# Recurrence scan: K and B in one stationary tile, V over U, 128x128 turns

## The reference, cut to what matters

```python
def step(state, inp):
    r_t, w_t, k_t, v_t, a_t, b_t = inp
    sa = jnp.einsum('bhvk,bhk->bhv', state, a_t)
    state = (state * w_t[:, :, None, :] + sa[..., None] * b_t[:, :, None, :]
             + v_t[..., None] * k_t[:, :, None, :])
    return state, jnp.einsum('bhvk,bhk->bhv', state, r_t)
...
y = rwkv7_scan(rh, heads(decay), kh, vh, -kk, kk * ah)
```

## Time and profile before

| what | value |
|---|---|
| median of 3 runs | 4486.77 us (4481.82 to 4492.76) |
| the profiled execution, its own time | 4486.94 us |
| span of the profiled execution | 4485.2 us |
| PE busy | 4139.9 us, 92% of the span |
| the two scans | 456 to 678 us and 1793.5 to 2015.5 us, 222 us each |

### The profile page before, as it was taken

One profiled execution on the slowest core, in us unless ns is written; L12 is line 12 of the kernel. 1 busy time (PEld: TensorE's weight loads), 2 busy tenths in 40 slices (PEclk: granted clock), 3 DMA queues, 4 the chain that ended last, 5 costly groups with the idle time before them and its releaser, 6 DMA issues.

```text
span 4485.2 us, 74522 instructions
## 1 busy us (share of the span) xinstructions
PE 4139.9 (92%) x32508; PEld 3239.7 (72%) x32508; DVE 1952.9 (44%) x2997; ACT 1514.7 (34%) x2697; POOL 548.8 (12%) x384
## 2 busy tenths in 40 slices
PE   7998779899998999789899989987899999999999
PEld 5676776677776776776677767755788888667877
DVE  5536335455345536335455344357432232443232
ACT  3533233333333533233333343257221121343221
POOL 1215101011002216001011001012000000150000
PEclk9999899999998999899999999999999999999999
DMA  4122002244322132003244321100111111101222
GB/s 161 39 104 71 31 4 104 80 170 173 136 82 103 48 104 66 32 9 114 93 169 169 128 80 43 52 24 1 38 62 62 63 65 57 57 6 66 94 94 85
DMA packets 97684, 351.74 MB, mean 78 GB/s; under 512 B 10064, under 2 KB 13648, under 8 KB 95952
## 3 DMA queue, kind: packets, MB, share of 16 engines
q1 hardware_dynamic: 86480, 313.02, 20.2%
q10 hardware_dynamic: 10880, 33.96, 2.1%
HBM read 332.26 MB, written 14.68 MB: 77 GB/s over the span
## 4 chain that ended last, share of the span: by engine, by line
PE 81%; DVE 8%; issue 3%; POOL 3%; ACT 3%; DMA 0%; ACTq 0%; DVEq 0%; SPq 0%; POOLq 0%
PE ps L350 20%; PE ps L351 19%; PE ps L353 19%; PE ps L1373 7%; PE ps L2414 1%; PE ps L1932 1%; DVE wlo L307 1%; DVE sml L2489 1%; POOL e L2948 1%; PE ps L391 1%; ACT whi L297 1%; PE ps L2861 1%; POOL dd L1215 1%; POOL ops L1231 1%; PE ps L885 1%
## 5 line engine op out<-in xcount | busy, mean ns | idle before, releaser
L307 DVE TENSOR_TENSOR wlo<-ring,whi 128x1024 fp32r<-128x1024 f32 x494 | 622.6, 1261 | 1827.8 <-ACT whi L297 1827.5
L297 ACT CAST whi<-ring 128x1024 fp32r<-128x1024 f32 x494 | 517.2, 1048 | 2069.2 <-PE ps L353 1791.7
L350 PE MATMUL ps<-h_hi,whi 128*128 128x512 f32 x1424 | 592.8, 416 | 21.6 <-DVE h_lo L461 10.2
L351 PE MATMUL ps<-h_lo,whi 128*128 128x512 f32 x1424 | 566.4, 398 | 0.0
L353 PE MATMUL ps<-h_hi,wlo 128*128 128x512 f32 x1424 | 566.0, 397 | 0.0
L350 PE MATMUL ps<-hm_hi,whi 128*128 128x512 f32 (+1 forms) x1408 | 514.6, 365 | 15.9 <-DVE hm_lo L464 14.4
L351 PE MATMUL ps<-hm_lo,whi 128*128 128x512 f32 (+1 forms) x1408 | 481.0, 357 | 0.0
L353 PE MATMUL ps<-hm_hi,wlo 128*128 128x512 f32 (+1 forms) x1408 | 418.9, 355 | 0.0
L350 PEld LDWEIGHTS ps<-h_hi,whi 128*128 128x128 f32 x1424 | 271.3, 191 | 141.8 <-issue 49.5
L350 PE MATMUL ps<-ac_hi,whi 128*128 128x512 f32 x880 | 330.5, 376 | 3.4 <-DVE wlo L307 3.4
L350 PEld LDWEIGHTS ps<-hm_hi,whi 128*128 128x128 f32 x1408 | 267.2, 190 | 85.9 <-DVE hm_lo L464 19.4
(11 more groups left out here) (386 smaller groups left out, 7240.6 us busy)
## 6 DMA issues: line engine op xcount, KB each, us to landing
ring<-in_w SPq DMA_DIRECT2D x590, 512.0 KB, 3.3
h_spill<-h ACTq DMA_DIRECT2D x2, 2048.0 KB, 6.7
x_spill<-x ACTq DMA_DIRECT2D x2, 2048.0 KB, 13.8
m_spill<-m ACTq DMA_DIRECT2D x2, 2048.0 KB, 9.8
h_again<-h_spill ACTq DMA_DIRECT2D x2, 2048.0 KB, 9.0
ma<-m_spill ACTq DMA_DIRECT2D x2, 2048.0 KB, 9.9
x<-x_spill ACTq DMA_DIRECT2D x2, 2048.0 KB, 9.9
x<-in_x SPq DMA_DIRECT2D x4, 512.0 KB, 7.8
```

Source lines behind the costliest of these rows:

```text
L297: self.A.copy(self.hi[k % 2][:], raw).then_inc(self.s_cut_hi.h, 1)
L307: self.V.tensor_tensor(self.lo[k % 2][:], raw, self.hi[k % 2][:].bitcast(F32), ALU.subtract).then_inc(self.s_cut_lo.h, 1)
L350: T.matmul(ps[:, b, 0:cw], hi, xh(q, c0, cw), start=q == 0, stop=False, skip_group_check=True)
L351: T.matmul(ps[:, b, 0:cw], hi, xl(q, c0, cw), start=False, stop=False, skip_group_check=True)
```

## The change

K and B are stored next to each other, chunk by chunk, in `kb`, so that one stationary tile of 64 rows by 128 columns holds both. One product then gives K and B with R and A for one head half, at place 0, in place of `ba` and `ka`. V moves to the fourth part of `ops` and A to the fifth. `stacked` contracts over 128 rows: the turned K and B stand under each other in `kbt`, and V and U in `vu`, so `st` and `yy` are one product each. `turned` turns whole 128x128 tiles with PE's transpose; the V tile holds two chunks, and is turned for each of them. `turned` and `stacked` and the new first product issue all their matmuls in one step of the weave. `tb` moves from place 1 of the old chunk to place 7 of the new one. PSUM banks 1 and 3 change roles. ACT gains the copy `ka` and a second copy for U, DVE masks in two halves, and POOL gains a mask of 64 rows by 512. The wait for the store of `m` moves from ACT to DVE, to the first V column. The other hunks write the same operands through views by chunk.

```diff
@@ -101,10 +101,10 @@
...
-SCAN_ACROSS = Order("ba rr tb st yy tv ka", "rr tb st yy")
-SCAN_ACT = Order("tx rr tb x2 y4 y8 u gp yy tv", "rr tb u yy")
-SCAN_DVE = Order("my ot a1 x4 p2 a2 p3 a3 p4 st stp mk", "a1 a2 a3 st stp")
-SCAN_POOL = Order("pw", "")
+SCAN_ACROSS = Order("kb rr st yy tv tb", "rr st yy")
+SCAN_ACT = Order("ka tx rr x2 y4 y8 u gp yy tv tb", "rr u yy")
+SCAN_DVE = Order("my ot rk a1 x4 p2 a2 p3 a3 p4 st stp", "a1 a2 a3 st stp")
+SCAN_POOL = Order("km pw", "")
...
@@ -1021,8 +1021,8 @@
...
-        R, K, Vv = self.r_k_v()
-        AT, BB, BON = ops[:, 3 * DT:4 * DT, :], ops[:, 4 * DT:5 * DT, :], self.X
+        R, kb, Vv, AT = self.scan_parts()
+        K, BB, BON = kb[:, :, :, 0, :], kb[:, :, :, 1, :], self.X
...
@@ -1182,9 +1182,11 @@
...
-                dst = low[:, j, :] if p is None else ops[:, DT * p + j, :]
+                dst = by_chunk(low[:, j, :] if p is None else R[:, j, :] if p == 0 else Vv[:, j, :]) if p != 1 else K[:, j]
                 mu = self.p1("mu_low", j) if p is None else self.p1("mu_rkv", DT * p + j)
-                V.scalar_tensor_tensor(dst, dd[n % 2][:], mu, zb[n % 2][:, 1:S + 1], ALU.mult,
+                if p == 2 and j == 0:
+                    V.wait_ge(self.s_st_m.h, self.s_st_m.n)
+                V.scalar_tensor_tensor(dst, by_chunk(dd[n % 2][:]), mu, by_chunk(zb[n % 2][:, 1:S + 1]), ALU.mult,
...
@@ -1262,9 +1264,11 @@
...
+        kb = self.view("kb", A1 + 4096, DT, NCH, 2, CH)
+        return ops[:, 0:DT, :], kb, ops[:, 3 * DT:4 * DT, :], ops[:, 4 * DT:5 * DT, :]
...
@@ -1377,6 +1382,22 @@
...
+        def stacked(bank, lt, rh, begin=True, signal=None):
+
+            for j in range(GP):
+                for u in range(2):
+                    i = T.matmul(ps[64 * u:64 * u + 64, 4 * g + bank, j * CH:(j + 1) * CH], m[lt][:, GP * g + j, u, :],
+                                 m[rh][:, GP * g + j, u, :], start=begin and j == 0, stop=True, skip_group_check=True)
+            i.then_inc(signal, 1)
+            yield False
+
+        def turned(bank, tile_of, signal):
+
+            for j in range(GP):
+                i = T.transpose(ps[:, 4 * g + bank, j * P:(j + 1) * P], tile_of(GP * g + j), self.c("ident"))
+            i.then_inc(signal, 1)
+            yield False
+
...
@@ -1403,33 +1424,40 @@
...
-                dve(c - 1, "mk")
-                yield from product("tt", 1, 0, CH, (mat("kar", 1), mat("vt")), signal=sp)
+                T.wait_ge(self.s_sg2[g].h, base[3] + SCAN_POOL.after(c - 1, "km"))
+                for j in range(GP):
+                    for u in range(2):
+                        i = T.matmul(ps[64 - 64 * u:128 - 64 * u, 4 * g + 3, j * CH:(j + 1) * CH],
+                                     m["ka"][0:64, GP * g + j, u, :], m["vu"][0:64, GP * g + j, u, :], start=j == 0,
+                                     stop=True, skip_group_check=True)
+                    if j == GP - 1:
+                        i.then_inc(sp, 1)
+                    yield False
...
-                dve(c, "ot")
-                yield from product("tt", 0, 0, CH, (mat(b, 1), X))
-                yield from product("tt", 0, 256, CH, (X, mat(b, 1)), signal=sp)
+                dve(c, "rk")
+                yield from product("tt", 0, 0, CH, (mat("ba"), X))
+                yield from product("tt", 0, 256, CH, (X, mat("ba")), signal=sp)
...
                 act(c, "rr")
-                yield from product("tt", 1, 0, CH, (mat("gp", 0), mat("rr")), signal=sp)
+                yield from product("tt", 3, 0, CH, (mat("gp", 0), mat("rr")), signal=sp)
...
@@ -1475,45 +1501,48 @@
...
-                yield from product("dt", 0, 0, 2 * CH, (raw(4, c), r_and_a(c)), signal=sx)
+                if old:
+                    act(c - 1, "tb")
+                for j in range(GP * g, GP * g + GP):
+                    for u in range(2):
+                        d, col = slice(64 * u, 64 * u + 64), 2 * CH * (j - GP * g)
+                        i = T.matmul(ps[:, 4 * g + u, col:col + 2 * CH],
+                                     m["kb"][d, j, c].rearrange("p x s -> p (x s)"),
+                                     ops[d, j:j + 4 * DT + 1:4 * DT, at], start=j == GP * g, stop=True,
+                                     skip_group_check=True)
+                i.then_inc(sx, 1)
+                yield False
...
-                yield from product("dt", 1, 0, CH, (raw(3, c - 1), mat("st")), begin=False, signal=sx)
-                yield from product("dt", 3, 0, CH, (raw(4, c - 1), eye))
-                yield from product("dt", 3, 256, CH, (raw(1, c - 1), eye), signal=sx)
+                yield from product("dt", 3, 0, CH, (raw(4, c - 1), mat("st")), begin=False, signal=sx)
...
-                act(c, "tb")
                 act(c, "u")
                 if new:
                     act(c, "y8")
-                yield from product("td", 0, 0, CH, (mat("bkt", 0), mat("u")), (mat("bkt", 1), mat("vt")), signal=sx)
+                yield from stacked(0, "kbt", "vu", signal=sx)
...
-                yield from product("td", 1, 0, CH, (mat("u"), mat(before, 0)), (mat("vt"), mat("kar", 0)), begin=False,
-                                   signal=sx)
+                yield from stacked(3, "vu", f"kr{(c - 1) % 2}", begin=False, signal=sx)
...
                 dve(c, "p4")
-                yield from product("dt", 2, 0, CH, (raw(2, c), eye), signal=sx)
+                yield from turned(2, lambda j: ops[:, 3 * DT + j, P * (c // 2):P * (c // 2) + P], sx)
                 act(c, "gp")
-                yield from product("dt", 3, 0, 2 * CH, (raw(1, c), r_and_a(c)), signal=sx)
+                yield from turned(1, lambda j: m["kb"][:, j, c].rearrange("p x s -> p (x s)"), sx)
...
@@ -1533,18 +1562,26 @@
...
+            if new:
+                if old:
+                    own(c, "ra")
+                across(c, "kb")
+                A.copy(m["ka"][0:64, mine, :, :].rearrange("p j u c -> p u j c"),
+                       ps[0:64, 4 * g:4 * g + 2, :].rearrange("p u (j c) -> p u j c", c=2 * CH)[:, :, :, CH:2 * CH]
+                       ).then_inc(sa, 1)
...
                 across(c, "rr")
-                A.copy(m["rr"][:, mine, :], one(1)).then_inc(sa, 1)
-                across(c, "tb")
-                A.copy(m["bkt"][:, mine, :, :], two(3)).then_inc(sa, 1)
+                A.copy(m["rr"][:, mine, :], one(3)).then_inc(sa, 1)
...
@@ -1561,19 +1598,22 @@
...
-                A.copy(m["u"][:, mine, :], one(1)).then_inc(sa, 1)
+                A.copy(m["vu"][64:128, mine, 0, :], one(3)[64:128])
+                A.copy(m["vu"][64:128, mine, 1, :], one(3)[0:64]).then_inc(sa, 1)
...
                 across(c, "tv")
-                A.copy(m["vt"][:, mine, :], one(2)).then_inc(sa, 1)
+                A.copy(m["vu"][0:64, mine, :, :], heads(2)[64 * (c % 2):64 * (c % 2) + 64]).then_inc(sa, 1)
+                across(c, "tb")
+                A.copy(m["kbt"][:, mine, :, :], heads(1)).then_inc(sa, 1)
...
@@ -1596,21 +1636,28 @@
...
-                across(c, "ba")
-                V.tensor_tensor(wide(b), both(0), mask("m_ba", 2 * CH), ALU.mult).then_inc(sv, 1)
-                V.tensor_tensor(m["oe"][:, mine, 0, :], both(0)[:, :, CH:2 * CH], mask("m_offT", CH),
+                across(c, "kb")
+                for u in range(2):
+                    i = V.tensor_tensor(m["ba"][64 - 64 * u:128 - 64 * u, mine, :], both(u)[64:128, :, CH:2 * CH],
+                                        mask("m_ba", 2 * CH)[64:128, :, CH:2 * CH], ALU.mult)
+                i.then_inc(sv, 1)
+                for u in range(2):
+                    i = V.tensor_tensor(m["oe"][64 - 64 * u:128 - 64 * u, mine, 0, :], both(u)[64:128, :, CH:2 * CH],
+                                        mask("m_offT", CH)[64:128], ALU.mult)
+                i.then_inc(sv, 1)
+                V.wait_ge(self.s_sa[g].h, base[1] + SCAN_ACT.after(c, "ka"))
+                V.tensor_tensor(m[f"kr{c % 2}"][:, mine, :, :].rearrange("p j u c -> p u j c"),
+                                ps[:, 4 * g:4 * g + 2, :].rearrange("p u (j c) -> p u j c", c=2 * CH)[:, :, :, 0:CH],
+                                self.c("m_ka", CH).unsqueeze(1).unsqueeze(1).to_broadcast([P, 2, GP, CH]),
                                 ALU.mult).then_inc(sv, 1)
...
@@ -1645,17 +1692,19 @@
...
-            if new:
-                across(c, "ka")
-                V.tensor_tensor(wide("kar"), both(3), mask("m_ka", 2 * CH), ALU.mult).then_inc(sv, 1)
 
...
+        before = self.c("m_ka", 2 * CH)[0:64, CH:2 * CH].unsqueeze(1).unsqueeze(1).to_broadcast([64, GP, 2, CH])
         for c in range(NCH + 1):
             yield
+            if c < NCH:
+                G.wait_ge(self.s_sa[g].h, base[1] + SCAN_ACT.after(c, "ka"))
+                G.tensor_tensor(m["ka"][0:64, mine, :, :], m["ka"][0:64, mine, :, :], before,
+                                ALU.mult).then_inc(self.s_sg2[g].h, 1)
...
```

(27 more changed lines are left out.)

55 lines of the change are left out of this document (26 added, 29 removed).

## The result

The changed kernel takes 4559.4 us, the median of four runs, against 4485.4 us for the kernel before: a ratio of 1.0157, 95% interval 1.0135 to 1.018. One of the four took 7143.5 us at a granted clock of 0.66; the ratio leaves it out, and the median of the other three is 4555.8 us. So the kernel is slower, by 70 us where 37 were forecast.

What follows compares the result with a forecast made beforehand. PE was taken as the bound, instruction supply nearly explaining its 25.0 us round. The new round: 24.0 array time and switches, 3.1 waits, 0.2 stops, 27.3 us; over 8 rounds and 2 scans +37, giving 4524 us, range 4465 to 4565.

Steps and rivals of the forecast that it cites:

- Instructions removed: PE in the scan: matmul records per round fall from 800 to 624, giving 4992 records and 39 instruction packets per scan.
- Stops of "issue": PE running out of instructions at blocks of 256: near 3 us per round, of which 2.8 go and 0.2 stay.
- the rival by which the stops stay: Stops are not a matter of instruction count and stay at 3 us: round 30.1, +82 us, 4569 us; chance 0.06.
- Array time and shape changes: PE streaming per round: 19.6 us becomes 24.0, with 10.4 of products and 1.6 of ten shape switches per group-chunk.
- Wait (a), `kbt`: The first product waits for ACT's `tb` copy, made last at place 7: 1.25 us, once per round.
- (b), U: PE's wait for U, now two ACT copies instead of one: 0.7 us per round, where it was 1.1.
- (c), `zz`: PE's wait for ACT `zz`: stays at 0.37 us per round.
- (d), `kar`: PE's wait for DVE `kar`, 0.86 us per round before: goes, since `ra` now needs older results.
- Wait (e), DVE's masks: Five DVE mask pieces at place 0 delay the other group's additions `p3`, `p4`: PE waits 0.75 us per round, bounds 0 and 1.3.
- Start and end of a scan: Outside the steady rounds, gains and losses alike: taken as 0, bounds -2 and +3 us.
- waits take over: Rival: ACT and DVE orders make 5 us of waits per round, switches cost 0.20; round 30.0, about 4555 us; chance 0.20.
- Switches are cheap: Rival: instruction supply was the bound and shape switches cost little, so faster: 4472 us, or 4452 with wait (a) hidden; chance 0.18.

Runs made afterwards that it cites:

- before_split: The kernel before, with each 128-column product of `product` issued as two of 64 columns: 4529.0 us, ratio 1.0087.
- before_turns: The kernel before, with the interleaving of PE's two sides off, all own steps issued before all across steps at each place: 4523.6 us, ratio 1.0089.
- split_turns: The changed kernel, with each of a group-chunk's eight transposes made a step of its own, other-group steps between them: 4609.3 us, ratio 1.0269.
- one_step: The changed kernel, with place 7's `yy`, turned V and turned K/B issued in one piece, no other-group step between: 4542.3 us, ratio 1.0119.
- dve_late: The changed kernel, with DVE's `oe` and `kr` mask pieces moved from place 0 to place 1, behind the other group's additions: 4520.3 us, ratio 1.0075.

## Why the prediction was right in sign and half the size

Step by step, in the prediction's terms. All sizes are those of the scans in the traces, 74 us where 37 were forecast:

- **Instructions removed.** 4992 PE records per scan, forecast and there (the groups of the scan's lines add up to it; the window of 261 us holds 4995). 39 instruction packets were forecast; the first scan has 40 of 0.66 MB. Right.
- **Stops of "issue".** 2.8 of 3 us per round were to go, and the steady rounds show none between blocks of 256. before_split and before_turns test the reason both ways. Right; the rival by which the stops stay is refuted, though its 4569 us lies near the result, nearer than the forecast's 4524. By the Trainium skill, "Runtime: NRT & Kernel Launch", section "Instruction fetch mechanics", the crossing of a block is mostly hidden. At 27.26 us per round the trace agrees; in the kernel before, at 25, it does not, and the 16 blocks that before_split adds, free by this rule, cost 40 us.
- **Array time and shape changes.** 24.0 us per round were forecast, with ten changes per group-chunk at 0.16. The array time is the round less its waits. Counted from starts at the pace of the earlier trace rows, as in the stretches above, the waits of a round are 1.5 for `p4`, 0.8 for `p3`, 0.9 for `kbt` and 0.75 for `vu` (a change of shape taken off the last two), and 0.4 and 0.3 ahead of two `zz` products: 4.7 us in all, up to 0.2 more apiece than the idle time that the view gives. That leaves 29.3 - 4.7 = 24.6. The changes cost 0.14 us (this timeline), 0.13 (split_turns) and 0.15 (one_step), so they were taken 0.4 too dear. The sum also had 0.82 for a product of 128 columns, read from the weight loads, where the matmuls take 0.88: 0.24 too little in four products. The Trainium skill, "TensorEngine Tiling (Array Packing)", section "Key Properties", has a change of tiling mode drain TensorE; the trace agrees, and here is its price. Array time and stops together, 24.2 forecast, are short by 0.4 us per round, 7 us in all; behind this number, with the two errors set right, stand some 0.8 us per round that were not taken apart. The mechanism is right, the size in part by errors that cancel.
- **Wait (a), `kbt`.** Forecast 1.25 us once per round, measured 0.9 (6.3 us in 7 times). Right. **(b), U:** 0.7 forecast, 0.7 measured (4.9 us in 7 times). **(c), `zz`:** 0.37 forecast in all; there are two, 0.4 and 0.3 from start to start. **(d), `kar`:** gone, as forecast.
- **Wait (e), DVE's masks: the step that failed.** The prediction wrote "I take 0.75, bounds 0 and 1.3". It is two waits per round, one for `p4` (1.27 us of idle matmuls, 8.9 us in 7 times) and one for `p3` (0.7, from 5.4 us in 8 times), 2.0 together, or 2.3 from start to start: outside the bounds either way. The mechanism, five pieces ahead of the other group's additions, was named rightly, and they take 2.4 us in the trace where 2.3 were reckoned. What the prediction took for one partly hidden wait comes in both halves of the round: the groups are four places apart, so each group's masks meet the other's additions, `p4` in one half and `p3` in the other. Its own sign of being wrong in size, "if DVE's longer chain stalls PE more often than once per round", came true. Mis-sized by 1.55 us per round, 25 us of the 37 missing; the waits for `zz` and `kbt` miss by 0.3 each, in opposite directions. dve_late takes this wait away and shortens the scans by 34 us; most of the wait for `vu` goes with it, and a wait for `kr` comes.
- **Start and end of a scan.** Taken at 0, measured 37.1 - 8 x 4.5 = +1 us per scan, 2 in all, inside the bounds. The round of before was taken as 25.0 where it is 24.8, 3 us in all.

25 + 7 + 2 + 3 = 37 us is the miss; since the array time was found by subtraction, that the sum closes proves nothing about its parts, and what is shown by an experiment of its own is wait (e). Of the rivals, "waits take over" (4555) gave almost the measured time and had nearly the measured waits, 4.7 us per round where it wanted 5, though its changes of shape were dearer (0.20) than they are. It was given a chance of 0.20. "Switches are cheap" fell with split_turns.

## What to carry to other kernels

Fewer instructions help only where PE stops for them; ask then what the new shapes take away. Here products on quadrants of the array ran beside each other, and products on whole rows or columns did not, so 22% fewer records took more array time. Where a change of shape has a price, put products of one shape next to each other, and stop interleaving across shapes. And when a piece of work grows on an in-order queue shared by two staggered groups, go through both halves of the round: each has its own victim. Moving the pieces one place later was worth 34 us here, more than the change gained in its best version.

## What was not expected of the hardware

- The stops for instructions depend on the pace. At 3.7 to 4.1 us per 256 PE instructions there is a stop at each block, at 4.36 us per block there was one of the matmuls in a whole scan. Splitting products in two at equal columns cost 40 us in the kernel before. A packet of instructions is on its way for only some 1.2 us (before_turns: 6 packets in 27.26 us, 1.7% of 16 engines), so the transfer alone does not make the 3.9 us per block; no run shows what does.
- A change of tile shape costs 0.13 to 0.15 us whichever way it goes (64x64 to 128x64 or 128x128 and back), and it adds up: 24 more per round were 49 us. Two blocks of transposes behind each other, with none between, took 0.50 us for the first four (one_step, starts at 598.89 and 599.39), where with a change on both sides of it the block took 0.59.
